# One step of a conformer and sparse-attention trunk on one core: the input norm cut into token tiles between the key/value products

## The chip, the core and the metric

The kernel runs on one core of a Trainium2 chip. Times are device microseconds (us) of one execution; lower is better. The core has five engines that run their own instruction streams and meet at semaphores: PE (matrix products and transposes, results in PSUM), DVE (vector work), ACT (pointwise functions, and here also an issuer of DMAs), POOL (vector work and software-issued DMAs) and SP (here only an issuer of DMAs). DMAs of all issuers run on the same 16 DMA engines; the trace lists the queue of SP as q1, that of ACT as q10 and that of POOL as q0.

## The reference, cut to what matters

One layer is computed for 512 prompt tokens and 64 sample tokens, all in float32. The change is about its first lines: the norm of the input, and the projection of the normed input to keys and values.

```python
def rms_norm(x, g):
    xf = x.astype(jnp.float32)
    y = xf * lax.rsqrt(jnp.mean(xf * xf, axis=-1, keepdims=True) + EPS)
    return (y * g.astype(jnp.float32)).astype(x.dtype)
...
    u, q, kc, vc, ks, vs, kw, vw, ng, mg = jnp.split(xn @ w_in, cuts, axis=-1)
...
        mix_p, st_p = mixer_prompt(rms_norm(h_p, g_mix[l]), w_in[l], conv_w, cmp_w, w_nsa_out[l], w_o[l])
        h_p = h_p + mix_p
        h_p = h_p + hier_moe(rms_norm(h_p, g_ffn[l]), *moe_w)
```

Everything behind it (gated convolution, three-branch attention over caches and windows, merge, 32 experts, final norm) needs the normed input, transposed to have the 1024 model columns on the partitions.

## The kernel before

The 576 tokens lie in five tiles: four of 128 tokens and one of 64. The 1024 columns lie in eight blocks of 128. PSUM is used as four slots of 1024 columns; each piece of PE work that goes through a slot is a job, and the list ORDER gives the jobs their slots in rotation. A job claims its slot (waits until the job before it there has been read), fills it, and its reader gives it back. The list has no say in the order of an engine's instructions: that is written out by hand in one block for each engine.

The start of the program runs in stages, each of them over all five tiles.

- SP issues the loads of the five tiles of x into h (lines 548 to 550), waits until all have landed (s_x, line 551), and then issues the key/value weights wkv (1024 x 792 values, one DMA, line 552), the convolution's taps and state, and the first four GLU weights (line 559).
- ACT issues three small loads (ident, mhalf, gmix; the list firsts, semaphore s_first, line 1005). gmix is the norm's gain as a 128 x 8 array: 1024 words of 4 bytes that each lie apart. Then it waits for all of x, squares the five tiles with a running sum (line 1010), takes half of the norm's results out of PSUM (line 1014), and issues 25 loads of constants (line 1017, semaphore s_const).
- POOL waits for all of firsts and for the five sums, raises the five columns to the power -1/2 in one instruction (scales, lines 775 and 776), waits for all constants, and then issues twelve small loads of the page table (line 816), two moves of cached window rows and one of the convolution's state from HBM to HBM (lines 818 and 820). Behind them come the rotations of the keys (rope, lines 832 to 837, once per tile and in two halves), after the second of them the gathers of cached rows (strides, line 850).
- DVE scales the five tiles (line 1282) and takes the other half of the norm's results out of PSUM, times gmix (line 1286).
- PE waits for firsts and for all five scaled tiles, transposes them (line 1831), one job for each block of columns, with all five tiles in it, and then multiplies with wkv (line 1855, one job kv for each tile; line 1860 for the tile of 64), which ACT takes out of PSUM (line 1023). A float32 product of 512 columns appears in the trace as two passes.

PE then turns the convolution's state (line 1870), does the GLU products (line 1839) and turns the gathered rows (line 1899) and the rotated keys (line 1888).

Of the kernel before, what the change touches and what calls it, by code (L numbers as in the profile page):

```python
# [11 lines left out]
ALU = mybir.AluOpType  # L12
# [4 lines left out]
P = 128  # L17
D = 1024
KD = D // P
# [46 lines left out]
ORDER = [("norm", k) for k in range(KD)] + [("kv", i) for i in range(NT)] + ["cst", "wdw"]  # L66
# [52 lines left out]
def build(nc, a):  # L119
    o = a["outs"]  # L120
    with ExitStack() as ctx:
        def sem(name):
            return ctx.enter_context(nc.semaphore(name))
# [34 lines left out]
        def take(eng, *jobs, it=None, per=0):  # L158

            highest(eng, filled, [want(j, it, per, 1) for j in jobs])  # L160
# [213 lines left out]
        s_wkv = sem("s_wkv")  # L374
# [172 lines left out]
        def _(sp):  # L547
            for i in range(QT):
                sp.dma_start(h[:, i, :], a["x_prompt"][0, i * P:(i + 1) * P, :]).then_inc(s_x, 16)
            sp.dma_start(h[0:NS_TOK, QT, :], a["x_sample"].rearrange("b t d -> (b t) d")).then_inc(s_x, 16)  # L550
            sp.wait_ge(s_x, 16 * NT)
            sp.dma_start(wkv, w_in_v[:, :, KV0:KV0 + KVN]).then_inc(s_wkv, 16)
# [15 lines left out]
            take(sp, JOB["norm", KD - 1])  # L568
# [194 lines left out]
        def on(t, i):  # L763
            return slice(0, TS[i])
# [7 lines left out]
        def scales(pool, st, n):  # L772

            pool.wait_ge(s_sq, NT * (n + 1))
            st.do(nc.gpsimd.tensor_scalar(rs[:, n, 0:NT], ss[:, n, 0:NT], 1.0 / D, EPS, ALU.mult, ALU.add))
            nc.gpsimd.tensor_tensor(rs[:, n, 0:NT], rs[:, n, 0:NT], mhalf[:, 0:NT], ALU.pow).then_inc(s_pow, 1)

# [26 lines left out]
        def _(pool):  # L804
# [7 lines left out]
            scales(pool, st, 0)  # L812
            pool.wait_ge(s_const, ALL_CONST)
# [6 lines left out]
            pool.dma_start(o["conv_s"][0, :, 0:PAD - DS, :], a["state_conv"][0, :, DS:PAD, :]).then_inc(s_moved, 16)  # L820

# [31 lines left out]
            take(pool, JOB["norm", KD - 1])  # L853
# [148 lines left out]
        def _(act):  # L1002
# [4 lines left out]
            act.wait_ge(s_x, 16 * NT)  # L1007
            act.wait_ge(s_pads, 1)
            for i in range(NT):
                nc.scalar.activation(xs[on(xs, i), i, :], h[on(h, i), i, :], ACT.Square, accum_out=ss[on(ss, i), 0, i:i + 1]).then_inc(s_sq, 1)  # L1010
            for k in range(1, KD, 2):
                j = JOB["norm", k]
                take(act, j)
                give(nc.scalar.activation(xT[:, k, :], slot(j)[:, 0:T], ACT.Copy, scale=gmix[:, k:k + 1]), j)  # L1014
# [260 lines left out]
        def _(dve):  # L1275
# [3 lines left out]
            dve.wait_ge(s_pow, 1)  # L1279
            for i in range(NT):  # L1280
                r = on(h, i)
                V.tensor_scalar(xs[r, i, :], h[r, i, :], rs[r, 0, i:i + 1], None, ALU.mult).then_inc(s_xs, 1)
            for k in range(0, KD, 2):
                j = JOB["norm", k]
                take(dve, j)
                give(V.tensor_scalar(xT[:, k, :], slot(j)[:, 0:T], gmix[:, k:k + 1], None, ALU.mult), j)
# [324 lines left out]
            def scaled(i):  # L1611
                dve.wait_ge(s_pow, 1 + i + 1)
                r = on(h, i)
                V.tensor_scalar(xs2[r, i, :], h[r, i, :], rs[r, 1, i:i + 1], None, ALU.mult).then_inc(s_xs, 1)

            dve.wait_ge(s_x, 16 * 2 * NT)
# [190 lines left out]
            def final(i):  # L1807
                dve.wait_ge(s_pow, 1 + NT + i + 1)
                r = on(h, i)
                V.scalar_tensor_tensor(h[r, i, :], h[r, i, :], rs[r, 2, i:i + 1], gfin[r, :], ALU.mult, ALU.mult).then_inc(s_final, 1)  # L1810
# [11 lines left out]
        def _(pe):  # L1822
# [3 lines left out]
            def norm_transposes(j0, src):  # L1826
                for k in range(KD):
                    claim(pe, j0 + k)
                    for i in range(NT):
                        n = TS[i]  # L1830
                        last = tr(slot(j0 + k)[:, i * P:i * P + n], src[0:n, i, k * P:(k + 1) * P], ident[0:n, 0:n])  # L1831
                    fill(last, j0 + k)

# [9 lines left out]
            pe.wait_ge(s_xs, NT)  # L1843
            norm_transposes(JOB["norm", 0], xs)

            for k in range(KD - 4, KD):
                result_of(pe, JOB["norm", k])
            pe.wait_ge(s_wkv, 16)
            for i in range(NT):
                j = JOB["kv", i]  # L1850
                claim(pe, j)
                if i < QT:
                    for lo, hi in ((0, 512), (512, KVN)):
                        for k in range(KD):
                            last = mm(slot(j)[:, lo:hi], xT[:, k, i * P:(i + 1) * P], wkv[:, k, lo:hi], start=k == 0, stop=k == KD - 1)  # L1855
                else:
                    half = KVN // 2
                    for k in range(KD):
                        for b in range(2):
                            last = mm(slot(j)[b * NS_TOK:(b + 1) * NS_TOK, b * 512:b * 512 + half], xT[:, k, SEQ:T], wkv[:, k, b * half:(b + 1) * half],  # L1860
                                      start=k == 0, stop=k == KD - 1)
                fill(last, j)

# [578 lines left out]
```

## Time and profile before

| what | value |
|---|---|
| time, median of 3 runs | 910.57 us (909.29 to 913.3) |
| the profiled execution: its own time | 911.5 us |
| the profiled execution: span from first to last instruction | 909.7 us |
| PE busy | 770.4 us, 85% |
| DVE, ACT, POOL busy | 41%, 25%, 19% |
| mean granted PE clock | 0.938 of 2.4 GHz |
| first PE instruction | 20.97 us |

The span is what the views count in; what lies around it in the profiled execution is 1.8 us. Times in the rows are from the span's start.

### The profile page before, as it was taken

Reading aid. Unit: us, or ns where it says so; the run is one execution under the profiler, and the core shown is the slowest. Engines: PE = TensorE matmul, PEld = TensorE weight load, DVE = VectorE, ACT = ScalarE, POOL = GpSimd, SP = SyncE. Lnnn points to the kernel's source line nnn. Section 1 sums busy time; section 2 is a strip of 40 time slices with the busy share of each in tenths; the row PEclk is TensorE's granted clock in tenths of the full one; section 3 lists DMA queues with packets and bytes.
Section 4 is the critical chain, followed back from the end, with each engine's and each line's share of the span. In section 5 each row is a group of like instructions: output and inputs, shape, how many; then the busy total and the mean of one; then the engine's idle time right before and its main releaser. Section 6 shows DMA issues by size and latency. Waiting matters only on the chain.

```text
span 909.7 us, 11093 instructions
## 1 busy us (share of the span) xinstructions
PE 770.4 (85%) x4293; PEld 526.7 (58%) x4293; DVE 373.1 (41%) x742; ACT 223.4 (25%) x477; POOL 173.2 (19%) x271
## 2 busy tenths in 40 slices
PE   0999999998989989999898879999991599988710
PEld 0555778584756667777666667754551456554500
DVE  1100598999778861030044532222237222221135
ACT  2101223252256651251243410001010012211121
POOL 1075625210100013000024200010000213221112
PEclk9999999999999999999999989999995599998965
DMA  8759535240210015522134289011137289999663
GB/s 276 160 4 298 143 90 134 96 128 1 64 53 2 1 30 158 166 66 70 47 93 140 80 241 363 1 49 79 47 146 281 84 316 412 407 400 398 241 229 115
DMA packets 91126, 138.95 MB, mean 153 GB/s; under 512 B 29209, under 2 KB 64153, under 8 KB 89911
## 3 DMA queue, kind: packets, MB, share of 16 engines
q1 hardware_dynamic: 71967, 103.77, 33.2%
q0 software_dynamic: 11392, 32.71, 12.3%
q10 hardware_dynamic: 7712, 1.72, 1.0%
q8 instruction: 36, 0.59, 0.3%
q14 instruction: 19, 0.16, 0.1%
HBM read 132.00 MB, written 21.14 MB: 168 GB/s over the span
## 4 chain that ended last, share of the span: by engine, by line
PE 69%; DVE 8%; DMA 8%; issue 6%; SPq 4%; ACT 2%; POOL 1%; POOLq 0%; DVEq 0%; ACTq 0%
PE ps L1839 17%; PE ps L2011 13%; PE ps L2254 6%; DMA keep<-w_up 6%; PE ps L1855 5%; PE ps L2323 4%; PE ps L1918 3%; SPq L640 3%; PE ps L2054 2%; PE ps L2029 2%; PE ps L2042 2%; PE ps L2339 1%; PE ps L1831 1%; PE ps L1899 1%; PE ps L2202 1%
## 5 line engine op out<-in xcount | busy, mean ns | idle before, releaser
L2011 PE MATMUL ps<-xT,keep 128*128 128x288 f32 x512 | 126.9, 407 | 0.8 <-ACT h L1178 0.4
L2011 PEld LDWEIGHTS ps<-xT,keep 128*128 128x128 f32 x512 | 96.5, 190 | 27.3 <-ACT h L1178 0.6
L1839 PE MATMUL ps<-xT,arena 128*128 128x288 f32 x384 | 95.4, 407 | 0.0
L1309 DVE SCALAR_TENSOR_TENSOR cv<-keep,cv 128x512 f32<-128x512 f32 x120 | 83.6, 747 | 1.4
L1839 PEld LDWEIGHTS ps<-xT,arena 128*128 128x128 f32 x384 | 72.1, 190 | 19.2
L2254 PE MATMUL ps<-arena,xT 128*128 128x512 f32 x128 | 55.5, 593 | 1.8 <-issue 1.8
L2323 PE MATMUL ps<-keep,mgT 128*64 128x256 f32 x288 | 45.7, 427 | 8.9 <-DMA keep<-w_up 7.6
L1855 PE MATMUL ps<-mgT,xT 128*128 128x512 f32 (+1 forms) x128 | 45.7, 521 | 1.1 <-ACT xT L1014 1.1
L2254 PEld LDWEIGHTS ps<-arena,xT 128*128 128x128 f32 x128 | 24.1, 190 | 31.4 <-issue 31.4
L2323 PE MATMUL ps<-arena,mgT 128*64 128x256 f32 x256 | 39.5, 409 | 3.1 <-DMA arena<-w_up 2.9
L792 ACT ACTIVATE mgT<-ps 64x512 f32<-64x512 f32 x56 | 33.2, 592 | 32.2 <-PE ps L1899 31.6
L980 POOL DMA_INDIRECT yscratch<-cv,slots_of x19 | 19.0, 999 | 110.4 <-PE ps L2313 76.5
L2323 PEld LDWEIGHTS ps<-keep,mgT 128*64 128x64 f32 x288 | 28.2, 154 | 20.2 <-issue 11.3
L1236 ACT ACTIVATE keep<-h 128x1024 f32<-128x1024 f32 (+1 forms) x5 | 5.3, 1058 | 136.3 <-DVE h L1621 127.7
L935 POOL TENSOR_SCALAR keep<-keep,pmod 128x64 f32<-128x64 f32 x16 | 6.8, 448 | 165.4 <-PE ps L2054 86.9
L1248 ACT ACTIVATE cv<-ps 128x128 f32<-128x128 f32 x19 | 5.3, 278 | 134.1 <-PE ps L2323 134.1
L1855 PEld LDWEIGHTS ps<-mgT,xT 128*128 128x128 f32 x128 | 25.3, 199 | 21.3 <-issue 18.5
L1785 DVE TENSOR_TENSOR arena<-ps,cv 128x128 f32<-128x128 f32 x19 | 5.5, 292 | 74.3 <-ACT cv L1248 74.3
L1839 PE MATMUL ps<-cv,keep 128*128 128x288 f32 x128 | 34.1, 422 | 0.7 <-DVE oT L1549 0.7
L1102 ACT ACTIVATE mgT<-ps 128x288 f32<-128x288 f32 x32 | 13.2, 411 | 83.7 <-PE ps L2011 83.5
L1119 ACT ACTIVATE arena<-ps,arena 128x128 f32<-128x128 f32 (+3 forms) x64 | 33.0, 527 | 1.5 <-DVE arena L1431 0.7
L1918 PE MATMUL ps<-mgT,arena 128*128 128x512 f32 x64 | 29.6, 622 | 3.9 <-DVE mgT L800 3.9
(377 smaller groups left out, 1283.9 us busy)
## 6 DMA issues: line engine op xcount, KB each, us to landing
arena<-w_down SPq DMA_DIRECT2D x21, 512.0 KB, 16.4
keep<-w_gate SPq DMA_DIRECT2D x18, 512.0 KB, 11.5
keep<-w_up SPq DMA_DIRECT2D x18, 512.0 KB, 17.2
keep<-w_in SPq DMA_DIRECT2D x16, 512.0 KB, 3.8
arena<-w_gate SPq DMA_DIRECT2D x14, 512.0 KB, 8.4
arena<-w_up SPq DMA_DIRECT2D x14, 512.0 KB, 12.8
h<-x_prompt SPq DMA_DIRECT2D x8, 512.0 KB, 5.4
arena<-w_in SPq DMA_DIRECT2D x8, 512.0 KB, 6.4
```

The source lines that it names most:

```text
L640: sp.dma_start(wgu[x % HOMES_W][:, n:n + 1, :, :].rearrange("p e k f -> p e (k f)"), a[name][0, expert_of(x) if e is None else e].rearrang ...
L792: last = copy(XT[q * HD:(q + 1) * HD, g, k0:k0 + KD // 2, (u // 2) * P:(u // 2 + 1) * P], v, *how)
L980: pool.indirect_dma_start(a["yscratch"][0:2 * T, :], bass.IndirectOffsetOnAxis(ap=slots_of[:, 1, blocks_of(p):blocks_of(p) + 1], axis=0), ...
L1119: nc.scalar.activation(x.prob[:, g, k], x.scores[:, g, k], ACT.Exp, bias=x.stat(0)[:, g, b:b + 1], accum_out=x.stat(1)[:, g, b:b + 1]).the ...
L1309: V.scalar_tensor_tensor(cv[:, c, 0:SEQ], aP[:, c, k:k + SEQ], wdw[:, c, k:k + 1], cv[:, c, 0:SEQ], ALU.mult, ALU.add).then_inc(s_tap[c], 1)
L1839: last = mm(tokens(j)[:, b, :], weights(k), halves(x[:, k, :])[:, b, :], start=k == 0, stop=k == n_k - 1)
L1855: last = mm(slot(j)[:, lo:hi], xT[:, k, i * P:(i + 1) * P], wkv[:, k, lo:hi], start=k == 0, stop=k == KD - 1)
L1918: last = mm(slot(j)[:, g * 512:(g + 1) * 512], w1[:, k, :], XT[:, g, k, 0:STR_S], start=k == 0, stop=k == KD - 1)
L2011: last = mm(out[:, 0:half], wmg[n // 2 % 3][:, k, :], xT[:, k, (n % 2) * half:(n % 2 + 1) * half], start=k == 0, stop=k == KD - 1, skip_gr ...
L2029: mm(x.scores[:, g, b * x.nk:(b + 1) * x.nk], qrot[hd, x.c, qc], kT[hd, br, 0:x.nk], start=b == 0, stop=False, skip_group_check=True)
L2254: last = mm(slot(j)[:, lo:lo + 512], xT[:, k, i * P:(i + 1) * P], wo[:, k, lo:lo + 512], start=k == 0, stop=k == KD - 1)
L2323: last = mm(slot(j + 1)[u * BR:(u + 1) * BR, 0:2 * F], xeT[p % 2][:, k, u * BR:(u + 1) * BR], wgu[(2 * p + u) % HOMES_W][:, :, k, :], star ...
```

## The change

Five things are moved, all in the first 110 us of the program.

- The jobs of the norm are cut by token tile and no longer by block of columns: one job holds the eight blocks of one tile. PE's order becomes: tile 0 and tile 1 turned, products of tile 0, tiles 2 and 3 turned, products of tile 1, tile 4 turned, products of tiles 2, 3 and 4.
- x has a semaphore for each tile, so ACT squares a tile as it lands, POOL raises one column at a time (scales_by_tile, which two later norms use already), and DVE scales a tile and takes a turned tile out of PSUM in one instruction each, the gain gmix spread along the tokens. ACT no longer takes any of the norm out of PSUM.
- The weights wkv are loaded in four parts of two column blocks, each issued behind one tile of x; the wait for all of x goes. PE waits for a part when tile 0's products come to it.
- ACT issues the 25 constants right behind the five squares.
- POOL waits for the four weight parts ahead of the page table's loads, and for the constants only behind the moves, ahead of the first rotation.

```diff
-ORDER = [("norm", k) for k in range(KD)] + [("kv", i) for i in range(NT)] + ["cst", "wdw"]
+ORDER = [("norm", 0), ("norm", 1), ("kv", 0), ("norm", 2), ("norm", 3), ("kv", 1), ("norm", 4), ("kv", 2), ("kv", 3), ("kv", 4), "cst", "wdw"]
...
             for i in range(QT):
-                sp.dma_start(h[:, i, :], a["x_prompt"][0, i * P:(i + 1) * P, :]).then_inc(s_x, 16)
-            sp.dma_start(h[0:NS_TOK, QT, :], a["x_sample"].rearrange("b t d -> (b t) d")).then_inc(s_x, 16)
-            sp.wait_ge(s_x, 16 * NT)
-            sp.dma_start(wkv, w_in_v[:, :, KV0:KV0 + KVN]).then_inc(s_wkv, 16)
+                sp.dma_start(h[:, i, :], a["x_prompt"][0, i * P:(i + 1) * P, :]).then_inc(s_x_tile[i], 16)
+                sp.dma_start(wkv[:, 2 * i:2 * i + 2, :], w_in_v[:, 2 * i:2 * i + 2, KV0:KV0 + KVN]).then_inc(s_wkv[i], 16)
+            sp.dma_start(h[0:NS_TOK, QT, :], a["x_sample"].rearrange("b t d -> (b t) d")).then_inc(s_x_tile[QT], 16)
...
             pool.wait_ge(s_first, 16 * len(firsts))
-            scales(pool, st, 0)
-            pool.wait_ge(s_const, ALL_CONST)
+            scales_by_tile(pool, st, 0)
+            for n in range(KD // 2):
+                pool.wait_ge(s_wkv[n], 16)
             for dst, src in idx_loads:
...
             pool.dma_start(o["conv_s"][0, :, 0:PAD - DS, :], a["state_conv"][0, :, DS:PAD, :]).then_inc(s_moved, 16)
+            pool.wait_ge(s_const, ALL_CONST)
...
-            act.wait_ge(s_x, 16 * NT)
             act.wait_ge(s_pads, 1)
             for i in range(NT):
+                act.wait_ge(s_x_tile[i], 16)
                 nc.scalar.activation(xs[on(xs, i), i, :], h[on(h, i), i, :], ACT.Square, accum_out=ss[on(ss, i), 0, i:i + 1]).then_inc(s_sq, 1)
-            for k in range(1, KD, 2):
-                j = JOB["norm", k]
-                take(act, j)
-                give(nc.scalar.activation(xT[:, k, :], slot(j)[:, 0:T], ACT.Copy, scale=gmix[:, k:k + 1]), j)
...
+            def row_scaled(i):
+                dve.wait_ge(s_pow, i + 1)
                 r = on(h, i)
                 V.tensor_scalar(xs[r, i, :], h[r, i, :], rs[r, 0, i:i + 1], None, ALU.mult).then_inc(s_xs, 1)
-            for k in range(0, KD, 2):
-                j = JOB["norm", k]
+
+            def row_turned(i):
+                j, n = JOB["norm", i], TS[i]
                 take(dve, j)
-                give(V.tensor_scalar(xT[:, k, :], slot(j)[:, 0:T], gmix[:, k:k + 1], None, ALU.mult), j)
+                g = gmix[:, :].unsqueeze(2).to_broadcast([P, KD, n])
+                give(V.tensor_tensor(xT[:, :, i * P:i * P + n], slot(j).rearrange("p (k c) -> p k c", c=P)[:, :, 0:n], g, ALU.mult), j)
...
+            def keys_values(i):
                 j = JOB["kv", i]
+                result_of(pe, JOB["norm", i])
                 claim(pe, j)
                 if i < QT:
                     for lo, hi in ((0, 512), (512, KVN)):
                         for k in range(KD):
+                            if i == 0 and lo == 0 and k % 2 == 0:
+                                pe.wait_ge(s_wkv[k // 2], 16)
```

SP's queue before: x first, then a wait, then the weights in one piece.

```order
L549 DMA h<-x_prompt 128x1024 x4
L550 DMA h<-x_sample 64x1024
L552 DMA mgT<-w_in 128x8x792 [waits s_x]
L554 DMA arena<-w_dw 31x512
L555 DMA arena<-state_conv 120x2x512
L559 DMA arena<-w_in 128x8x128 x4
```

And now (mgT<-w_in is a weight part):

```order
L550 DMA h<-x_prompt 128x1024
L551 DMA mgT<-w_in 128x2x792
L550 DMA h<-x_prompt 128x1024
L551 DMA mgT<-w_in 128x2x792
...
L552 DMA h<-x_sample 64x1024
L554 DMA arena<-w_dw 31x512
L555 DMA arena<-state_conv 120x2x512
L559 DMA arena<-w_in 128x8x128 x4
```

Nothing in the queue waits any more: tiles of x and weight parts alternate, four of each (two are shown), and the last tile, the taps, the state and the GLU weights follow at once.

PE before, from its first instruction on (emptied0 to emptied3 are the four slots given back, s_xs counts the scaled tiles):

```order
L1831 MATMUL ps<-ident,arena 128x128 [waits s_xs,s_first]
L1831 MATMUL ps<-ident,arena 128x128 x3
L1831 MATMUL ps<-ident,arena 128x64
...
L1855 MATMUL ps<-mgT,xT 128x512 [waits emptied3,s_wkv,emptied2,emptied0,emptied1]
L1855 MATMUL ps<-mgT,xT 128x512 x7
L1855 MATMUL ps<-mgT,xT 128x280 x8
L1855 MATMUL ps<-mgT,xT 128x512 [waits emptied1]
```

And now:

```order
L1844 MATMUL ps<-ident,arena 128x128 [waits s_xs,s_first]
L1844 MATMUL ps<-ident,arena 128x128 x7
L1844 MATMUL ps<-ident,arena 128x128 [waits s_xs]
...
L1856 MATMUL ps<-mgT,xT 128x512 [waits s_wkv0,emptied0]
L1856 MATMUL ps<-mgT,xT 128x512
L1856 MATMUL ps<-mgT,xT 128x512 [waits s_wkv1]
...
L1856 MATMUL ps<-mgT,xT 128x280 x8
L1844 MATMUL ps<-ident,arena 128x128 [waits s_xs]
L1844 MATMUL ps<-ident,arena 128x128 x7
L1844 MATMUL ps<-ident,arena 128x128 [waits emptied0,s_xs]
```

The first products of tile 0 stand behind 16 transposes and no longer behind all 40; the transposes of tiles 2, 3 and 4 stand between products. The first instruction waits for firsts as before.

POOL before, from the powers to the first rotation (s_pool is POOL's own step counter):

```order
L775 TENSOR_SCALAR rs<-ss 128x5 [waits s_sq,s_first]
L776 TENSOR_TENSOR rs<-rs,mhalf 128x5 [waits s_pool]
L816 DMA pidx<-page_table 64x1x1 [waits s_const]
L816 DMA pidx<-page_table 64x1x1 x7
L816 DMA pidx<-page_table 32x16x1 x4
L818 DMA out_k_win_s<-state_k_win 8x4x16128
L818 DMA out_v_win_s<-state_v_win 8x4x16128
L820 DMA out_conv_s<-state_conv 8x11264
L832 TENSOR_TENSOR arena<-keep 128x2x32 [waits emptied0]
```

And now:

```order
L777 TENSOR_SCALAR rs<-ss 128x1 [waits s_sq,s_first]
L778 TENSOR_TENSOR rs<-rs,mhalf 128x1 [waits s_pool]
...
L811 DMA pidx<-page_table 64x1x1 [waits s_wkv2,s_wkv3,s_wkv1,s_wkv0]
L811 DMA pidx<-page_table 64x1x1 x7
L811 DMA pidx<-page_table 32x16x1 x4
L813 DMA out_k_win_s<-state_k_win 8x4x16128
L813 DMA out_v_win_s<-state_v_win 8x4x16128
L815 DMA out_conv_s<-state_conv 8x11264
L828 TENSOR_TENSOR arena<-keep 128x2x32 [waits emptied2,s_const]
```

One pair of instructions for the powers has become five (one is shown), the first of which still waits for firsts, and the wait for the constants has moved from the page table's loads to the first rotation.

## Rows read from the trace of the kernel before

**Rows 1.** The page: shares of the chain that ended last, by engine

```profile
PE 69%; DVE 8%; DMA 8%; issue 6%; SPq 4%; ACT 2%; POOL 1%; POOLq 0%; DVEq 0%; ACTq 0%
```

**Rows 2.** That chain in order of time: start us, us, what

```profile
2.61 7.81 DMA h<-x_sample
...
10.44 5.32 ACT arena L1010 x10
...
16.21 1.20 POOL rs L776
...
17.43 3.41 DVE arena L1282 x5
...
20.97 10.78 PE ps L1831 x40
...
32.88 45.75 PE ps L1855 x128
...
101.15 0.87 PE ps L1899 x8
```

**Rows 3.** Timeline, ACT takes key/value tiles: start, us, engine line [idle before]

```profile
46.75 0.83 ACT L1023 ACTIVATE keep<-ps 128x792 f32<-128x792 f32 x1 [14.23 <-PE ps L1855]
...
57.39 0.83 ACT L1023 ACTIVATE keep<-ps 128x792 f32<-128x792 f32 x1 [9.81 <-PE ps L1855]
```

**Rows 4.** Two stretches of tile 0's products: length, PE busy (instructions), clock, DMA

```profile
34.20:37.60 3.40, 3.40 (x5) 1.00 0.90 93
39.40:42.80 3.40, 3.40 (x10) 1.00 0.71 210
```

**Rows 5.** DMA issues, first 10 us: count, KB, us to landing; timeline of gmix

```profile
h<-x_prompt SPq DMA_DIRECT2D x1, 512.0 KB, 3.9
...
gmix<-g_mix ACTq DMA_DIRECT2D x1, 4.0 KB, 8.9
...
1.69 0.46 ACTq L1005 DMA_DIRECT2D gmix<-g_mix  x1
```

**Rows 6.** DMA queues from 5.75 to 8.25: packets, MB, share of 16 engines

```profile
q1 hardware_dynamic: 274, 1.00, 100.0%
q10 hardware_dynamic: 269, 0.00, 6.1%
```

**Rows 7.** The same from 8.25 to 10.00

```profile
q10 hardware_dynamic: 759, 0.00, 27.7%
```

**Rows 8.** The same from 13.5 to 18.5, inside the weights' load

```profile
q1 hardware_dynamic: 660, 2.09, 103.2%
```

**Rows 9.** POOL's powers by tile in later norms: ns min/median/max

```profile
L783 POOL TENSOR_SCALAR rs<-ss x10: 190/192/1172, 622.1 to 898.3; 128x1 f32<-128x1 f32 x10
...
L784 POOL TENSOR_TENSOR rs<-rs,mhalf x10: 549/565/1596, 622.4 to 898.6; 128x1 f32<-128x1 f32 x10
```

**Rows 10.** DVE, groups by shape: a later norm's turned tile: busy us, mean ns

```profile
L1630 DVE TENSOR_TENSOR xT<-ps,gffn 128x1024 f32<-128x1024 f32 x4 | 4.9, 1218 | 0.7 <-PE ps L2267 0.7
```

**Rows 11.** Timeline, ACT issues the first and the last constants

```profile
31.78 1.16 ACTq L1017 DMA_DIRECT2D gffn<-g_ffn  x2
...
44.77 0.45 ACTq L1017 DMA_DIRECT2D pmod<-c_pmod  x1
```

**Rows 12.** Timeline, POOL: page table, first rotation, first index sum

```profile
46.79 7.37 POOL L816 DMA_DIRECT2D pidx<-page_table  x12 [29.40 <-DMA pmod<-c_pmod]
...
55.80 0.36 POOL L832 TENSOR_TENSOR arena<-keep 128x64 f32<-128x64 f32 x1
...
74.86 0.28 POOL L846 TENSOR_SCALAR gidx<-pidx,pmod 128x4 int32<-128x4 int32 x1 [10.64 <-DMA pidx<-page_table]
```

**Rows 13.** POOL's DMA issues: count, KB, median us to landing (issued 55.2, 53.5, 75.8)

```profile
out_conv_s<-state_conv POOLq DMA_DIRECT2D x1, 352.0 KB, 31.7
pidx<-page_table POOLq DMA_DIRECT2D x1, 2.0 KB, 21.3
...
arena<-cache_k_cmp,gidx POOLq DMA_INDIRECT x2, 14.6
```

More of the change, by code:

```diff
@@ L373, in build @@
         s_x = sem("s_x")
-        s_wkv = sem("s_wkv")
+        s_x_tile = [sem(f"s_x_tile{i}") for i in range(NT)]
+        s_wkv = [sem(f"s_wkv{n}") for n in range(KD // 2)]
         s_wring = [sem(f"s_wring{s}") for s in range(4)]
@@ L567, in _ @@
                 glu_weights(n)
-            take(sp, JOB["norm", KD - 1])
+            take(sp, JOB["norm", NT - 1])
             compress_weights("w_ck1")
@@ L770, in tokens @@
             return halves(slot(j))[:, :, 0:T // 2]
[L772 to L776, printed above, removed]
         def scales_by_tile(pool, st, n):
@@ L851, in strides @@
                                         bass.IndirectOffsetOnAxis(ap=gidx[:, r:r + 1], axis=0)).then_inc(s_raw[r % 2], 16)
-            take(pool, JOB["norm", KD - 1])
+            take(pool, JOB["norm", NT - 1])
             strides(0, 0)
@@ L1277, in _ @@
             V = nc.vector
-            dve.wait_ge(s_pow, 1)
-            for i in range(NT):
+            def row_scaled(i):
+                dve.wait_ge(s_pow, i + 1)
                 r = on(h, i)
                 V.tensor_scalar(xs[r, i, :], h[r, i, :], rs[r, 0, i:i + 1], None, ALU.mult).then_inc(s_xs, 1)
-            for k in range(0, KD, 2):
-                j = JOB["norm", k]
+            def row_turned(i):
+                j, n = JOB["norm", i], TS[i]
                 take(dve, j)
-                give(V.tensor_scalar(xT[:, k, :], slot(j)[:, 0:T], gmix[:, k:k + 1], None, ALU.mult), j)
+                g = gmix[:, :].unsqueeze(2).to_broadcast([P, KD, n])
+                give(V.tensor_tensor(xT[:, :, i * P:i * P + n], slot(j).rearrange("p (k c) -> p k c", c=P)[:, :, 0:n], g, ALU.mult), j)
+            row_scaled(0)
+            row_scaled(1)
+            row_turned(0)
+            row_scaled(2)
+            row_turned(1)
+            row_scaled(3)
+            row_scaled(4)
+            for i in (2, 3, 4):
+                row_turned(i)
             def gated(c):
@@ L1611, in scaled @@
             def scaled(i):
-                dve.wait_ge(s_pow, 1 + i + 1)
+                dve.wait_ge(s_pow, NT + i + 1)
                 r = on(h, i)
                 V.tensor_scalar(xs2[r, i, :], h[r, i, :], rs[r, 1, i:i + 1], None, ALU.mult).then_inc(s_xs, 1)
-            dve.wait_ge(s_x, 16 * 2 * NT)
+            dve.wait_ge(s_x, 16 * NT)
             def merged_out(i):
@@ L1807, in final @@
             def final(i):
-                dve.wait_ge(s_pow, 1 + NT + i + 1)
+                dve.wait_ge(s_pow, 2 * NT + i + 1)
                 r = on(h, i)
@@ L1824, in _ @@
             tr = nc.tensor.transpose
[L1826 to L1832, printed above, removed]
             def project(j, weights, x, n_k):
@@ L1842, in _, with row_turned @@
             pe.wait_ge(s_first, 16 * len(firsts))
[L1843 to L1849, printed above, removed]
+            def row_turned(i):
+                j, n = JOB["norm", i], TS[i]
+                pe.wait_ge(s_xs, i + 1)
+                claim(pe, j)
+                for k in range(KD):
+                    last = tr(slot(j)[:, k * P:k * P + n], xs[0:n, i, k * P:(k + 1) * P], ident[0:n, 0:n])
+                fill(last, j)
+            def keys_values(i):
                 j = JOB["kv", i]
+                result_of(pe, JOB["norm", i])
                 claim(pe, j)
@@ L1862, in _ @@
                 fill(last, j)
+            row_turned(0)
+            row_turned(1)
+            keys_values(0)
+            row_turned(2)
+            row_turned(3)
+            keys_values(1)
+            row_turned(4)
+            for i in (2, 3, 4):
+                keys_values(i)
             j = JOB["cst"]
```

## The prediction

> **What bounds the kernel now.** I read the chain that ended last first. PE holds 69% of it, and no other engine more than 8% [rows 1]. So a change at the start is worth what it moves PE's first long block of work, as long as everything that PE meets later is ready earlier too. In order of time the chain shows that PE stands still for 20.97 us and then does little until 32.88: the last tile of x lands at 2.61 + 7.81 = 10.42, ACT squares five tiles in 5.32, POOL raises to the power, DVE scales five tiles in 3.41, PE turns them in 10.78, and only then do the key/value products begin; from there PE runs without a gap to the first gathered rows at 101.15 [rows 2]. The stages follow each other instead of overlapping, so there are at most 32.88 us to win, less what one tile needs to pass through all of them.
>
> PE is also slow at first. Equal stretches of 3.40 us, both full of passes of 512 columns, hold 5 passes and then 10; the clock column says 1.00 in both, but a pass that takes twice as long ran at the lower level (1.2 GHz) and then at 2.4 [rows 4]. Tile 0's products so took 46.75 - 32.88 = 13.87 us, tile 1's 57.39 - 46.75 = 10.64 [rows 2, 3]. Most of the transposes before them ran slowly as well: 10.78 us for four and a half tiles is 2.40 us a tile, where eight transposes later take 0.87 [rows 2].
>
> **The change, part by part.** The new path to the first product is: gmix and tile 1 of x land, two powers, two scalings, 16 transposes.
>
> *When POOL may start.* The first power and the first transpose wait for all of firsts, and the last of these is gmix: issued at 1.69, landed 8.9 later, at 10.6 [rows 5]. Before, this was hidden, since the squares ended at 10.44 + 5.32 = 15.76 [rows 2]; now nothing hides it. And it will come later than 10.6. gmix is 1024 words, each a packet. While x streamed on SP's queue, ACT's queue sent 269 packets beside 274 of x in 2.5 us, one for one [rows 6]; the other 759 left in the next 1.75 us, mostly once x was through [rows 7]. In the changed kernel SP's queue does not run dry at 8.5: the weight parts lie between the tiles. Tiles have 128 packets and go at 274 / 2.5 = 110 per us [rows 6], parts have 256 and go at 660 / 5 = 132 alone [rows 8], some 125 with words between. A tile and a part are then 384 packets in 3.2 us, 120 per us. All 1600 packets take 13 us and end near 16, so the 759 words have company throughout: 759 / 120 = 6.3 us, the last at 14.6, landed about 0.6 later as before (10.0 against 10.6): **15.2**. The bounds are 10.6 (as before) and 18 (the words wait for the end of the stream at 16, then leave as in rows 7).
>
> The Trainium skill says otherwise on this ("DMA: Bandwidth & Descriptors", Queues, rings and completion order): an engine that alternates between queues drains a whole packet of some 9 to 17 descriptors from one before it switches. By that the 64 words of each engine would be gone in a few turns, long before 10.6; rows 6 count one for one, and I go by the rows.
>
> *From there to the first product.* A pair of power instructions for one column takes 0.19 + 0.55 us with short waits, 0.9 together, and 1.0 from the release on [rows 9]: 16.2. DVE scales tile 0 in 3.41 / 5 = 0.68 [rows 2]: 16.9. PE turns it in 2.40, at the slow rate, from 17.0 to 19.4, and tile 1 behind it to 21.8. Tile 1's scaling is ready at 17.8; in the longest case seen for the pair, 1.17 + 1.60 [rows 9], at 19.7, which would cost 0.3. DVE takes tile 0 out in 1.22 [rows 10], beside the second turn. The first product starts at **21.9** instead of 32.88: 11.0 us earlier.
>
> *Do the weights come?* Tile 0 of x lands at 0.74 + 3.9 = 4.6 [rows 5]; a part and a tile more are 3.2 us, so tile 1 lands at 7.8, tile 3 at 14.2, the last part at 16.2, tile 4 at 16.8. All lie ahead of 21.9, so the four waits for parts cost nothing; that cover is 5.7 us.
>
> *What is added to PE.* Tiles 2, 3 and 4 are turned between products: at most 3 x 0.87 = 2.6 us at the full clock [rows 2]. At the slow rate it would be 6.0, if the clock did not rise during tile 0's products. Before it rose about 6 us into them [rows 4], and I take the same 13.87 for tile 0. The bounds there are 10.64 (full at once, 3.2 less) and 21.3 (low throughout, 7.4 more). DVE takes tiles 2 to 4 out while PE multiplies, and ACT's four copies out of PSUM go; neither was on the path for longer than a us.
>
> *ACT's queue.* The 25 constants take 44.77 + 0.45 - 31.78 = 13.4 us to issue [rows 11]. Behind the squares they run from about 18 to 31.5; behind them waits the taking out of tile 0's products, due at 21.9 + 13.87 = 35.8. Cover: 4.3 us; beyond it PE would wait only when tile 4 is turned into that slot, over 12 us later.
>
> *POOL's queue.* Five pairs end near 20. Page table and moves are issued in 55.80 - 46.79 = 9.0 us [rows 12], to 29. Before, all constants had landed ahead of this; now the last of them are issued beside it. The moves ended at 55.2 + 31.7 = 86.9, 31.1 us after their issue [rows 12, 13]; so by 60 the queue of POOL is empty and the constants are in at the latest. Then two rotations, (74.86 - 10.64) - 55.80 = 8.4 us [rows 12], the index sums, about 1, and the first gather, 14.6 [rows 13]: 84. PE turns that gather at 101.15 before [rows 2], 8.4 us earlier now: 92.8. Cover: 8.7 us, so constants may land as late as 68.7 at no cost.
>
> **Sum.** -11.0 for the first product, +2.6 for the three turns: -8.4. The profiled execution took 911.5, its span 909.7; 911.5 - 8.4 = 903.1. It lies 0.9 above the median of 910.57, so in terms of the median I expect **902.2**. I know nothing later that would take the time back: the loads and gathers behind 101 us are released by PE's own progress.
>
> **Rivals.** *gmix is not late*, since ACT's words go several at a time between two long packets. Then tile 1 decides: landed 7.8, squared 1.06 [rows 2], 1.2 with its sum: 9.0, power 10.0, scaled 10.7, turned 13.1; first product at 13.2, 19.7 earlier, minus 2.6 is -17.1: 893.5. Against it: rows 6. This is what the Trainium skill's rule, told above, would give.
>
> *gmix is later still, or the gain is used up elsewhere:* the words wait for the GLU weights as well, which SP now issues right behind, some 10 us more; the first product comes at about 32 and the 2.6 us of turns are left, 911 to 913. Or the clock stays low through tile 0: 902.2 + 7.4 + 3.4 for slow turns is 913. The result is no change.
>
> *The constants starve, slower than before.* The last constants share the engines with the page table's words and the moves. If words and constants hold each other up for as long again as the table's load took, 21.3 us [rows 13], constants land at 81, 12.7 past the cover: 902.2 + 12.7 = 914.9 or a little more. It decides from 77 on (68.7 + 8.4). For it: one-for-one sharing as in rows 6, with slow neighbours. Against: POOL's queue drains however slowly ACT's goes, and then nothing is in the way.
>
> **How the numbers follow.** Forecast 0.70, gmix not late 0.11, gain used up 0.11, starved constants 0.08. The forecast's own spread comes from gmix (10.6 would give 897.6, 18 gives 905), the clock (-3.2) and the tenths of POOL, about 897 to 907. The range reaches down to the first rival: 893 to 907, which leaves out the other two. A measurement of this kernel can tell about 0.5%, 4.6 us, from no change: faster means below 906.0. Of the forecast nine tenths lie there, with the first rival 0.75; slower takes most of its rival, 0.08; the rest, 0.17, is the same.
>
> **What would show it.** In the changed profile: gmix lands near 15 and not near 10.6, and POOL's first power starts with it; first transposes near 17, first product near 22; 13 to 14 us for tile 0's products, with half-rate passes at first; ACT takes tile 0 out near 36 right as PE ends; PE goes without a gap from there; POOL's first rotation waits for a constant until some time in 45 to 60; PE's turn of the first gather near 93 without a wait. I am wrong if gmix lands by 11 (too much), if PE stands between products for scaled tiles or gathers, or if the time behind 101 us does not move along.

## The result, and the profile after

The changed kernel is slower. It takes 927.42 us (median of 4 runs, 923.95 to 930.76) against 910.84 (4 runs, one more than stood ahead of the prediction; 909.29 to 913.30) for the kernel before: a ratio of 1.0179, with a 95% interval of 1.0135 to 1.0224. The forecast was 902.2, with a range of 893 to 907, so the direction was wrong as well as the size. The profiled execution took 926.73, its span is 924.9 us, 15.2 more than before.

The chain that ended last, by engine and by line, first lines of that part of the page (the line that answers to [rows 1]):

```profile
PE 65%; DMA 9%; DVE 8%; issue 7%; ACTq 5%; SPq 2%; ACT 2%; POOL 1%; POOLq 0%; DVEq 0%
PE ps L1835 16%; PE ps L2022 12%; PE ps L2265 6%; ACTq L1009 5%; PE ps L2334 4%; DMA keep<-w_up 4%; PE ps L1929 3%; PE ps L1856 3%; DMA arena<-w_up 2%; PE ps L2065 2%; PE ps L2053 2%; PE ps L2040 2%; PE ps L2350 2%; DMA h<-x_sample 2%; SPq L640 1%
```

ACTq stood at 0% and now holds 5%, all of it on one line: L1009 is ACT's loop that issues the constants. An issuing loop has become part of what sets the end.

PE's timeline shows where (start, us, engine, line, operation; in brackets the idle time before and what ended it). It answers to the PE lines of [rows 2]. L1844 turns tiles of x, L1856 multiplies with wkv, and the last line is the start of the GLU products:

```profile
17.67 3.64 PE L1844 MATMUL ps<-ident,arena 128*128 128x128 f32 x16 [17.67 <-DVE arena L1274]
21.11 11.93 PE L1856 MATMUL ps<-mgT,xT 128*128 128x512 f32 x32
32.87 1.91 PE L1844 MATMUL ps<-ident,arena 128*128 128x128 f32 x16
34.62 10.80 PE L1856 MATMUL ps<-mgT,xT 128*128 128x512 f32 x32
70.03 1.08 PE L1844 MATMUL ps<-ident,arena 64*128 64x64 f32 x8 [24.61 <-ACT keep L1015]
71.05 23.28 PE L1856 MATMUL ps<-mgT,xT 128*128 128x512 f32 x64
...
101.05 9.24 PE L1835 MATMUL ps<-xT,arena 128*128 128x288 f32 x37
```

Until 45.42, when tile 1's products end, PE runs without a gap, as was forecast. Then PE wants to turn tile 4 into the slot that holds tile 0's keys and values, and ACT (L1015) has not taken these out: 24.61 us of standing. ACT was issuing the whole time. Its timeline, cut to the long issues (answers to [rows 3] and [rows 11]):

```profile
19.39 1.07 ACTq L1009 DMA_DIRECT2D gffn<-g_ffn  x2
...
30.08 6.69 ACTq L1009 DMA_DIRECT2D keep<-c_cosR  x1
36.80 1.50 ACTq L1009 DMA_DIRECT2D keep<-c_sinR  x1
38.32 7.43 ACTq L1009 DMA_DIRECT2D identb<-c_identb  x1
45.78 2.92 ACTq L1009 DMA_DIRECT2D causal<-c_causal  x1
...
51.10 7.07 ACTq L1009 DMA_DIRECT2D keep<-c_hsum  x1
58.21 6.30 ACTq L1009 DMA_DIRECT2D ovl<-c_ovl  x1
...
68.56 0.45 ACTq L1009 DMA_DIRECT2D pmod<-c_pmod  x1
69.06 1.55 ACT L1015 ACTIVATE keep<-ps 128x792 f32<-128x792 f32 x2 [48.52 <-issue]
```

The second column is the length of the issue instruction itself. Before, most of them took 0.45 to 0.65 us; here four take 6.3 to 7.4, and the loop lasts from 19.39 to 69.01: 49.6 us instead of 13.4. The profile shows no semaphore that ACT waits for ("<-issue"). ACT's own work, two copies of 0.8 us, stands behind it.

What else was on the DMA engines? The queues from 30 to 50 us, then from 50 to 62, then from 62 to 69 (packets, MB, share of 16 engines):

```profile
q0 software_dynamic: 170, 0.01, 76.4%
q10 hardware_dynamic: 405, 0.33, 5.0%
...
q0 software_dynamic: 127, 4.13, 92.4%
q10 hardware_dynamic: 121, 0.23, 5.5%
...
q10 hardware_dynamic: 1605, 0.48, 29.4%
q0 software_dynamic: 81, 0.36, 15.1%
```

q0 is POOL's queue: first the page table's words, then the moves. In the first stretch 170 of its packets, some 9 KB in all, take 76.4% of 16 engines' 20 us, which is 244 us of engine time. By the trace's packet records nearly all of it, 243 us, goes to 64 packets of 128 bytes, 8 KB together, at 3.6 to 4.4 us each; the other 106 packets take 1 us in sum. In the second the moves' long packets take 92.4%. ACT's queue (q10) sends 405 and 121 packets in these 32 us, and 1605 in the 7 us after them, when POOL's is nearly through. POOL's first power and its first rotation:

```profile
15.90 0.19 POOL L777 TENSOR_SCALAR rs<-ss 128x1 f32<-128x1 f32 x1 [13.73 <-DMA gmix<-g_mix]
...
70.78 0.32 POOL L828 TENSOR_TENSOR arena<-keep 128x64 f32<-128x64 f32 x1 [39.67 <-DMA pmod<-c_pmod]
```

**The balance on PE** sets the rows above against [rows 2, 3] and the start of the GLU products before:

```profile
85.36 15.79 PE L1839 MATMUL ps<-xT,arena 128*128 128x288 f32 x64
```

First product 21.11 instead of 32.88, -11.8; tile 0's products 11.8 instead of 13.9, -2.1; the two turns between products, each counted from its own start to the start of the products behind it, 1.75 and 1.02, +2.8; tile 1's products +0.2; the wait +24.6; the products of tiles 2 and 3 23.2 instead of 21.3, +1.9. That is +15.6; the GLU products begin 101.05 - 85.36 = 15.7 later, and the span is 15.2 longer. The last term is TensorE's clock: PE stood from 45.42, the granted clock was 0.53 from 50 to 60 and 0.50 from 60 to 70, and the first passes behind the wait ran at that lower level (1.2 GHz): 6 passes from 71 to 74 at 0.50, 9 from 77 to 80 at 1.00. The windows of 20 us from 20 on (length, PE busy and instructions, granted clock, DMA share, GB/s) show the hole:

```profile
20.00:40.00 20.00, 20.00 (x68) 1.00 0.94 108
40.00:60.00 20.00, 5.42 (x20) 0.77 0.96 210
60.00:80.00 20.00, 9.96 (x26) 0.64 0.37 96
80.00:100.00 20.00, 20.00 (x83) 1.00 0.38 132
```

### The profile page after: what moved, and what is told of

It is laid out like the page before. It is cut to its first block, busy times and chain, and to the rows that moved or that the text cites. A ratio compares the mean times of both kernels' runs of the same rounds, so it can differ in the third digit from the quotient of the medians.

```text
span 924.9 us, 11108 instructions
## 1 busy us (share of the span) xinstructions
PE 762.8 (82%) x4293; PEld 523.3 (57%) x4293; DVE 375.3 (41%) x743; ACT 220.9 (24%) x473; POOL 177.7 (19%) x279
## 4 chain that ended last, share of the span: by engine, by line
PE 65%; DMA 9%; DVE 8%; issue 7%; ACTq 5%; SPq 2%; ACT 2%; POOL 1%; POOLq 0%; DVEq 0%
PE ps L1835 16%; PE ps L2022 12%; PE ps L2265 6%; ACTq L1009 5%; PE ps L2334 4%; DMA keep<-w_up 4%; PE ps L1929 3%; PE ps L1856 3%; DMA arena<-w_up 2%; PE ps L2065 2%; PE ps L2053 2%; PE ps L2040 2%; PE ps L2350 2%; DMA h<-x_sample 2%; SPq L640 1%
## 5 line engine op out<-in xcount | busy, mean ns | idle before, releaser
L1856 PE MATMUL ps<-mgT,xT 128*128 128x512 f32 (+1 forms) x128 | 46.0, 520 | 0.0
L2265 PEld LDWEIGHTS ps<-arena,xT 128*128 128x128 f32 x128 | 24.1, 190 | 31.4 <-issue 31.4
L2334 PE MATMUL ps<-arena,mgT 128*64 128x256 f32 x256 | 36.7, 382 | 5.9 <-DMA xT<-w_up 3.0
L1844 PE MATMUL ps<-ident,arena 128*128 128x128 f32 (+1 forms) x40 | 6.6, 339 | 42.3 <-ACT keep L1015 24.6
L1856 PEld LDWEIGHTS ps<-mgT,xT 128*128 128x128 f32 x128 | 25.2, 200 | 19.9 <-issue 17.1
```

Source lines behind the costliest of these rows:

```text
L2265: last = mm(slot(j)[:, lo:lo + 512], xT[:, k, i * P:(i + 1) * P], wo[:, k, lo:lo + 512], start=k == 0, stop=k == KD - 1)
L2334: last = mm(slot(j + 1)[u * BR:(u + 1) * BR, 0:2 * F], xeT[p % 2][:, k, u * BR:(u + 1) * BR], wgu[(2 * p + u) % HOMES_W][:, :, k, :], star ...
```

## The experiments

Three theories were weighed. **A**: POOL's page-table words and moves keep ACT's packets from going out, ACT is held inside its issue instructions, and PE waits for ACT. **B**: it is SP's GLU weights, now issued earlier, that hold ACT. **C**: ACT's hold-up is beside the point, and it is the late landing of the constants (the first rotation needs them) that costs. All comparisons below were made with runs of the kernel before on the same chip, whose median was 912.6 us (23 runs) for the first four kernels and 912.1 (13 runs) for the last four.

### The constants ahead of the page table again

The smallest undoing: POOL's wait goes back, all else of the change stays.

```diff
             for n in range(KD // 2):
                 pool.wait_ge(s_wkv[n], 16)
+            pool.wait_ge(s_const, ALL_CONST)
             for dst, src in idx_loads:
...
-            pool.wait_ge(s_const, ALL_CONST)
```

> The changed kernel with one part undone: POOL waits for the constants ahead of the page table's loads again, so nothing of POOL's queue is on the DMA engines while ACT issues constants. Theory A (ACT's issue is blocked because its packets share the engines with POOL's page-table words and moves, so ACT cannot take tile 0 out of PSUM and PE stands 24.6 us ahead of tile 4's turn): ACT is through with the constants by about 34, takes tile 0 out by 35, PE has no gap above 1 us between 21 and the GLU products, and the time is 911.5 - 10.9 = 900.6, between 898 and 904. Theory B (the GLU weights that now flow at the same time block ACT's issue): ACT stays blocked past 45 and the time stays above 912.

Measured: 901.36 us (898.53 to 902.62, 4 runs), ratio 0.9876 (0.9844 to 0.9908). ACT's last issue, its first copy and PE's turn of tile 4, then POOL's page table, on their timelines:

```profile
35.39 0.45 ACTq L1009 DMA_DIRECT2D pmod<-c_pmod  x1
35.89 0.83 ACT L1015 ACTIVATE keep<-ps 128x792 f32<-128x792 f32 x1 [15.59 <-issue]
...
43.92 0.71 PE L1844 MATMUL ps<-ident,arena 64*128 64x64 f32 x8
...
39.26 7.38 POOL L812 DMA_DIRECT2D pidx<-page_table  x12 [17.56 <-DMA pmod<-c_pmod]
```

ACT is through at 35.84, 33 us sooner, and PE turns tile 4 without a gap. SP's weights were issued as in the changed kernel, and ACT's loop took 16.7 us beside them (19.16 to 35.84), 3.3 more than before, where the loop of the changed kernel took 36 more; so B falls. In the changed kernel, too, SP issued nothing between 25.89 and 71.15, while ACT's long issues ran from 30 on. Of the five parts of the change, this one wait turns a gain of 1.2% into a loss of 1.8%.

### One neighbour at a time

Two kernels leave one of POOL's two DMA groups early and put the other behind the wait for the constants. Moves late:

```diff
             for dst, src in idx_loads:
...
+            pool.wait_ge(s_const, ALL_CONST)
             for name, st_name in (("k_win_s", "state_k_win"), ("v_win_s", "state_v_win")):
...
-            pool.wait_ge(s_const, ALL_CONST)
```

> The changed kernel with the three moves put behind POOL's wait for the constants; the page table's loads stay ahead of it. Theory A with both neighbours at fault: four waves of page-table packets of about 5 us each, from 31 to 51, still block ACT, the moves no longer do: ACT takes tile 0 out near 53 instead of 69, PE waits some 8 us at tile 4: 907 to 911. If the moves alone were at fault: no gap, 899 to 903; if the page table alone: as the changed kernel, above 922.

Page table late, moves early:

```diff
-            for dst, src in idx_loads:
-                with nc.allow_non_contiguous_dma(reason="a few words"):
-                    pool.dma_start(dst, src).then_inc(s_idx, 16)
             for name, st_name in (("k_win_s", "state_k_win"), ("v_win_s", "state_v_win")):
...
             pool.wait_ge(s_const, ALL_CONST)
+            for dst, src in idx_loads:
+                with nc.allow_non_contiguous_dma(reason="a few words"):
+                    pool.dma_start(dst, src).then_inc(s_idx, 16)
```

> The changed kernel with the page table's loads put behind POOL's wait for the constants; the three moves stay ahead of it and so are issued at 22, beside the GLU weights. Theory A with both at fault: 64 packets of 2.4 to 2.9 us on 16 engines, about 12 us or a little more, from 24 to 38; ACT is through by 42 to 48 and PE waits 0 to 4 us at tile 4: 900 to 905. If the moves alone were at fault: as the changed kernel, above 920.

Measured: 913.47 us (911.23 to 916.59, 10 runs), ratio 1.0018 (1.0000 to 1.0035), with the moves late; 908.09 (906.0 to 908.79, 8 runs), ratio 0.9950 (0.9935 to 0.9965), with the table late. ACT's last issue and PE's turn of tile 4, in the one and in the other:

```profile
54.01 0.45 ACTq L1009 DMA_DIRECT2D pmod<-c_pmod  x1
...
55.49 1.08 PE L1844 MATMUL ps<-ident,arena 64*128 64x64 f32 x8 [10.45 <-ACT keep L1015]
```

```profile
48.44 0.45 ACTq L1009 DMA_DIRECT2D pmod<-c_pmod  x1
...
49.91 1.08 PE L1844 MATMUL ps<-ident,arena 64*128 64x64 f32 x8 [5.08 <-ACT keep L1015]
```

ACT ends its issues at 54.46 and 48.89. Against 35.84 with neither neighbour the page table's words cost 18.6 us and the moves 13.1; 35.84 + 18.6 + 13.1 = 67.5, where both together gave 69.01. So both hold ACT, their costs nearly add up, and the 10 KB of the page table (eight loads of 0.25 KB, four of 2 KB) cost more than the 4 MB of the moves.

Both times lie above the ranges that I had expected, by 2.5 and 3.1 us. The waits were longer (10.45 for some 8, 5.08 for 0 to 4), and I had no term for what follows a wait: the products of tiles 2 and 3 took 23.5 and 24.1 us, where the first experiment's kernel, without a wait, took 21.5.

### ACT spared, the constants late all the same

SP issues the constants instead of ACT, behind the GLU weights; POOL's order is that of the change.

```diff
-            for dst, src in consts:
-                with nc.allow_non_contiguous_dma(reason="small vectors, once"):
-                    act.dma_start(dst, src).then_inc(s_const, 16)
...
             for n in range(4):
                 glu_weights(n)
+            for dst, src in consts:
+                with nc.allow_non_contiguous_dma(reason="small vectors, once"):
+                    sp.dma_start(dst, src).then_inc(s_const, 16)
```

> The changed kernel with the 25 constants issued by SP, behind the GLU weights; POOL's order as in the change. The constants come as late as in the change, but another engine stands for them. Theory A (ACT held up in its issue): ACT takes tile 0 out at 33 to 34, no gap on PE at tile 4, SP stands until some 65 to 70 instead; the first rotation waits for the constants until then, the first gather lands near 70 + 24 = 94 and PE, there at about 90.5, waits some 4 us: 901 to 906. Theory C (it is the lateness of the constants for POOL and DVE that costs): no better than the changed kernel, 920 or more.

Measured: 912.01 us (908.03 to 914.94, 10 runs), ratio 0.9993 (0.9967 to 1.0020). That was missed: neither slow as under C nor fast as under A. ACT is free and PE turns tile 4 at 44.99 without a wait; the GLU products start 11.5 us earlier than before. But now SP is held. Its longest issue and its last one, POOL's first rotation, and two of PE's rows:

```profile
37.82 20.97 SPq L570 DMA_DIRECT2D b<-b_ck  x1
...
74.02 0.43 SPq L570 DMA_DIRECT2D pmod<-c_pmod  x1
...
75.80 0.32 POOL L831 TENSOR_TENSOR arena<-keep 128x64 f32<-128x64 f32 x1 [44.24 <-DMA pmod<-c_pmod]
...
91.08 1.09 PE L1910 MATMUL ps<-ident,arena 128*128 128x128 f32 x8 [1.39 <-DMA arena<-cache_k_cmp,gidx]
100.34 1.39 PE L1899 MATMUL ps<-ident,keep 128*128 128x128 f32 x5 [8.18 <-POOL keep L836]
```

One issue of a load of 0.2 KB took 21 us. The constants land at 75.8 and cost their own stall: 1.39 us for the first gather and 8.18 for the rotated keys, and PE comes out of it at the lower clock (the products behind it take 9.48 us instead of 8.03), so that the whole lead of 11.5 is gone. A is right that the issuer is held, whichever engine that is; C is right that lateness alone is expensive once PE is early.

### The same order of POOL in the kernel before

One part of the change alone: the old kernel, POOL's waits placed as in the change.

```diff
             scales(pool, st, 0)
-            pool.wait_ge(s_const, ALL_CONST)
+            pool.wait_ge(s_wkv, 16)
             for dst, src in idx_loads:
...
+            pool.wait_ge(s_const, ALL_CONST)
```

> The kernel before with one part of the change alone: POOL waits for the weights ahead of the page table's loads, and for the constants only ahead of the first rotation; ACT issues the constants where it did. Theory A (page-table words and moves keep ACT's queue from sending, so ACT stands in its issue instructions): ACT's last constant is issued near 65 to 70 instead of 44.8 and ACT takes tile 0 of the key/value products then instead of at 46.75. PE meets nothing of it, since its four slots hold tiles 0 to 3 until 78: about the time of before, 908 to 914. First rotation at 70 to 75, index sum near 80, the gather still ahead of 101. Theory C (lateness of the constants itself costs here as well): index sum at 84 or later, gathers past 101, 915 to 922. Against theory A: constants issued by 50 as before.

Measured: 910.97 us (909.02 to 914.37, 10 runs), ratio 0.9981 (0.9951 to 1.0011). ACT's timeline, its third issue and its next own work, then PE's products of all four tiles:

```profile
37.81 22.51 ACTq L1018 DMA_DIRECT2D bdw<-b_dw  x1
...
76.10 2.27 ACT L1024 ACTIVATE keep<-ps 128x792 f32<-128x792 f32 x3 [42.60 <-issue]
...
33.86 44.64 PE L1856 MATMUL ps<-mgT,xT 128*128 128x512 f32 x128 [1.14 <-ACT xT L1015]
```

ACT is held here too, until 76.05, with one issue of 22.5 us; that is 6 us longer than the 65 to 70 expected. It costs nothing, because the four slots take tiles 0 to 3 before PE needs one back (78.5). So the hold-up is not a matter of the new tiling. The new tiling makes it cost: it puts the turn of tile 4 behind the emptying of tile 0's slot, so that PE needs that slot at 45.4, 33 us earlier. The constants came even later than with SP as issuer (first rotation at 77.38, index sum at 85.88, past the 84 from which theory C expected a loss) and that was free as well: PE turned the first gather at 100.86 without a wait, since PE was not early.

### gmix: early, and with less beside it

The kernel of the first experiment leaves one term of the forecast that can be shortened: POOL starts at 15.66, when gmix lands, while tile 1 of x was squared from 8.36 on. First, gmix ahead of all on SP's queue, waited for by DVE alone:

```diff
-        firsts = [(ident[:, :], a["c_ident"]), (mhalf[:, :], a["c_mhalf"]), (gmix[:, :], a["g_mix"].rearrange("l (k p) -> p (l k)", p=P))]
+        firsts = [(ident[:, :], a["c_ident"]), (mhalf[:, :], a["c_mhalf"])]
...
+                sp.dma_start(gmix[:, :], a["g_mix"].rearrange("l (k p) -> p (l k)", p=P)).then_inc(s_gmix, 16)
             for i in range(QT):
...
+            dve.wait_ge(s_gmix, 16)
             row_scaled(0)
```

> The kernel with POOL's wait for the constants back ahead of the page table, and gmix issued first of all on SP's queue instead of ACT's, with a semaphore of its own for which DVE alone waits. Theory: in the kernel without this the start is set by gmix (landed 15.7) and not by x, whose tile 1 was squared at 8.4 already. Then gmix lands before tile 1 here; power near 10.4, tile 1 scaled near 11.1, turned by 13.6, first product at 13.5 to 14.5 instead of 20.8, parts of the weights still in time (the last is needed near 18.8): 893 to 896 us. Rival 1: the 1024 words at the head of SP's queue hold x up by as much as they are gained (a word for a turn each): tile 1 squared near 14, time as without the edit, 900 to 902. Rival 2: PE then stands for weight parts between tile 0's products, 897 to 900.

Measured: 892.48 us (889.67 to 893.91, 4 runs), ratio 0.9794 (0.9756 to 0.9832): the best kernel of the study. gmix in the table of DMA issues (count, KB, us to landing), and on the timelines POOL's first power and PE's first rows:

```profile
gmix<-g_mix SPq DMA_DIRECT2D x1, 4.0 KB, 2.4
```

```profile
7.97 0.19 POOL L780 TENSOR_SCALAR rs<-ss 128x1 f32<-128x1 f32 x1 [5.80 <-ACT arena L1009]
...
9.82 3.65 PE L1848 MATMUL ps<-ident,arena 128*128 128x128 f32 x16 [9.82 <-DVE arena L1277]
13.25 11.20 PE L1860 MATMUL ps<-mgT,xT 128*128 128x512 f32 x32
...
38.17 0.68 PE L1848 MATMUL ps<-ident,arena 64*128 64x64 f32 x8 [1.33 <-ACT keep L1018]
```

With nothing ahead of it gmix lands in 2.4 us instead of 14; the first product is 7.5 us earlier. ACT's constants, ending at 37.15, are now just late for PE: 1.33 us, the same wait of PE for ACT in small.

Second, the weight parts behind all five tiles of x, gmix on ACT's queue as in the change:

```diff
             for i in range(QT):
                 sp.dma_start(h[:, i, :], a["x_prompt"][0, i * P:(i + 1) * P, :]).then_inc(s_x_tile[i], 16)
-                sp.dma_start(wkv[:, 2 * i:2 * i + 2, :], w_in_v[:, 2 * i:2 * i + 2, KV0:KV0 + KVN]).then_inc(s_wkv[i], 16)
             sp.dma_start(h[0:NS_TOK, QT, :], a["x_sample"].rearrange("b t d -> (b t) d")).then_inc(s_x_tile[QT], 16)
+            for i in range(QT):
+                sp.dma_start(wkv[:, 2 * i:2 * i + 2, :], w_in_v[:, 2 * i:2 * i + 2, KV0:KV0 + KVN]).then_inc(s_wkv[i], 16)
```

> The kernel with POOL's wait for the constants back ahead of the page table, gmix left on ACT's queue, and the four weight parts issued behind all five tiles of x instead of among them. If gmix's words go one for one beside SP's packets, fewer packets lie beside them when x has gone out in 512 packets: gmix lands near 10.6 as in the kernel before, the power follows at 11.5, turns from 12.4 to 16.1, first product near 16.2 instead of 20.8, parts in by 18.2 (the last needed near 21.3): 896 to 898 us. If instead the words wait until SP's queue runs dry, gmix lands at 18 or later and the time is 902 to 905.

Measured: 901.79 us (898.68 to 902.15, 4 runs), ratio 0.9892 (0.9855 to 0.9930), no better than the kernel of the first experiment. My expectation was wrong, and the reason is that it forgot part of the stream: gmix's words go one for one beside SP's packets, and here SP's stream also does not end with x, since the parts follow without a wait. The queues from 4 to 14 us in the changed kernel, then from 4 to 16 in this one, and POOL's first power in this one:

```profile
q1 hardware_dynamic: 1196, 3.86, 98.2%
q10 hardware_dynamic: 1127, 0.01, 6.4%
```

```profile
q1 hardware_dynamic: 1283, 4.15, 98.3%
q10 hardware_dynamic: 1258, 0.02, 6.8%
```

```profile
16.51 0.19 POOL L778 TENSOR_SCALAR rs<-ss 128x1 f32<-128x1 f32 x1 [14.35 <-DMA gmix<-g_mix]
```

1127 packets of ACT's queue beside 1196 of SP's, and 1258 beside 1283. What order SP's packets have makes little difference (gmix landed 14.7 us after its issue here, 13.9 in the first experiment's kernel); that they go on does. In the kernel before gmix landed at 10.6, since SP waited there for x and its queue ran dry [rows 7].

Third, gmix first on SP's queue, with the order tiles 0 and 1, the four parts, tiles 2 to 4:

```diff
-            for i in range(QT):
+            for i in range(2):
                 sp.dma_start(h[:, i, :], a["x_prompt"][0, i * P:(i + 1) * P, :]).then_inc(s_x_tile[i], 16)
+            for i in range(QT):
                 sp.dma_start(wkv[:, 2 * i:2 * i + 2, :], w_in_v[:, 2 * i:2 * i + 2, KV0:KV0 + KVN]).then_inc(s_wkv[i], 16)
+            for i in range(2, QT):
+                sp.dma_start(h[:, i, :], a["x_prompt"][0, i * P:(i + 1) * P, :]).then_inc(s_x_tile[i], 16)
```

> As the kernel with gmix first on SP's queue, and on that queue the order tile 0 and tile 1 of x, the four weight parts, tiles 2, 3 and 4. If tile 1 sets the first product once gmix is early, it lands near 6.3, is squared by 8.1, scaled by 9.8, turned by 12.2: first product near 12.3, 1 to 1.5 us less than with parts among the tiles, 892 to 895 us. If the weight parts set it, no difference between the two; if the later tiles come too late to be turned between the products, PE waits there and it is slower than the other.

Measured: 894.25 us (891.47 to 898.48, 4 runs), ratio 0.9824 (0.9777 to 0.9870), the same as the first of these three within the spread of the runs. The time lies in the range that I had expected, but not for the reason given, a gain over the first of the three. Tile 1 was scaled 0.5 us earlier, but the turns of both tiles start with tile 0 (9.86 against 9.82) and run through in 3.65, so the first product comes at 13.30 against 13.25. Tile 1 did not set it.

## Why the prediction was wrong, point by point

**What held.** gmix lands late and starts the norm: 15.8 (issued 1.68, landed 14.1 later) against a forecast of 15.2, POOL's first power at 15.90, first transposes at 17.67 (17.0), first product at 21.11 (21.9). That the last of these comes out so close is in part luck: the start was 0.7 late, and the two turns took 3.4 us where 4.9 was written. The count of packets one for one carried the landing of gmix; the experiment with the parts behind x bore it out where my own expectation for it forgot it. So the first rival falls: 1127 words against 1196 rows is one for one, and in the 0.13 us from 8.00 on, the time of one row, the 16 engines sent 16 rows and 15 words. The Trainium skill ("DMA: Bandwidth & Descriptors", Queues, rings and completion order) has an engine drain a whole packet of some 9 to 17 descriptors from one queue before it switches; these counts do not agree with that. PE met no wait for a weight part. Tile 0's products took 11.8 us, between the fast bound of 10.64 and the 13.87 that the sum carried over. The turns between the products cost 2.8 us where 2.6 was written.

**The step that failed** is the paragraph on ACT's queue: "The 25 constants take 13.4 us to issue [rows 11]. Behind the squares they run from about 18 to 31.5." They took 49.6. The 13.4 us were measured where nothing of POOL's queue went out beside them, and were carried to a place where POOL's page table and moves go out beside it. The same paragraph named the right consequence ("PE would wait only when tile 4 is turned into that slot, over 12 us later"): the wait came there, and its size is 70.0, just behind the end of ACT's first copy (69.9), less 45.4: 24.6 us. The forecast had this wait at nothing.

The trace of before had both halves of this, and I read neither. SP's timeline there shows that an issuer can be held in its issue, and the queues from 54 to 74 us show that the page table and the first of the moves fill the engines:

```profile
13.32 14.32 SPq L559 DMA_DIRECT2D arena<-w_in  x4
```

```profile
q0 software_dynamic: 167, 1.04, 81.1%
```

Four issues took 14.3 us, while the 3.2 MB of key/value weights were queued ahead of them; and 167 packets took 81% of all engines for 20 us. Nothing else wanted the engines then, so it cost nothing.

**The third rival named the cause and not the path.** "The constants starve" was there, with a chance of 0.08, but priced through their landing and POOL's first rotation. The last of them landed by 70.78, when the rotation began, only 2.1 past the cover of 68.7, and by that path the time would have been about 904. ("By 60 the queue of POOL is empty", as the prediction has it, was wrong too: the last of its moves was issued at 30.55 and landed 37.3 later, at 67.9.) The path that decided ran through the issuer: a starved queue holds the engine that fills it, and what stands behind the loop on that engine. That words and constants meet was made certain by the moved wait; 0.08 was the chance for a cost that I looked for in the wrong place.

**The cover of the rotations was wrong too,** though this did not decide. It was taken from the first gather alone, and was to decide "from 77 on". With the constants at 75.8 and ACT free, PE lost 9.6 us in two waits, 8.2 of them for the rotated keys, which stand behind the gather in POOL's order and in no term of mine. The gather itself was issued at 85.28 there and awaited until 91.08: 5.8 us, where 14.6 was written.

**What the forecast described did come true in the kernel of the first experiment**: 901.36 against 902.2. In part by chance. Against runs of the kernel before on its own chip (912.6) that is 11.2 us less, where 8.4 was forecast: tile 0's products took 10.65 us there (20.79 to 31.44), the fast bound of the forecast and 3.2 less than its value. And of the 12.5 us by which the GLU products began earlier, the profiled span keeps 9.7: one later turn of gathered rows ran at a granted clock of 0.50 (3.61 us instead of 1.95), and the waits for expert weights from 640 us on were 3.5 us longer in sum (15.9 against 12.4). These two are more than the 2.8 lost; where the rest came back was not traced.

**What stays open.** Which resource holds the issue instruction: the runs show that ACT or SP is held while POOL's packets have the engines, and for how long; by what it is held inside the instruction they do not show. Nor is it shown why a 128-byte packet of the page table takes 3.6 us and more.

## What to carry to other kernels

An engine that issues DMAs is not done when it has come to the issue: while another queue keeps the DMA engines busy, the issue itself can last, and everything behind it in the program of that engine is late. So a duration for an issuing loop holds only for the traffic it was measured in; when a wait is moved, look at which transfers it kept apart. And when a stage is made earlier, recompute every cover against the new time of the one who needs it, for all that stands in the queue and not for the first item only.

## What the runs showed that I had not expected

- Single issues of small loads (0.2 and 2 KB) lasted 20.97 us on SP and 22.51 on ACT, where the same two took 0.54 and 0.46 us in the kernel before.
- 10 KB of page table held ACT longer (18.6 us) than 4 MB of moves (13.1 us): 64 packets of 128 bytes took nearly all of 76.4% of sixteen engines for 20 us.
- 1024 words of 4 bytes land in 2.4 us at the head of a queue and in 14 beside a stream, and the stream's order makes little difference to that (13.9 and 14.7).
- A wait on PE has a tail, and it does not grow with the wait: against 21.5 us in the first experiment's kernel, the products of tiles 2 and 3 took 24.1 behind a wait of 5.1 us, 23.5 behind 10.5 and 23.2 behind 24.6; behind a wait of 1.3 us they took 21.5, no more than without one.
